# Four unnormalised feed-forward tiles and thirteen earlier modulation dots in a two-block transformer kernel

## The reference

```
h = h + merged @ w_o
hn = rmsnorm(h, ffn_norm_g)
up = causal_dwconv(hn @ w_up, ffn_conv_w, ffn_conv_b)      # 3 taps over the tokens
val, gt = split(up);  h = h + (silu(gt) * val) @ w_down
```

## Time and profile before

| | us |
|---|---|
| median of 3 runs | 2860.99 |
| lowest, highest | 2860.46, 2868.71 |
| span of the profiled execution | 2867.0 |
| PE busy in it | 2802.2 |
| DVE busy in it | 2197.3 |
| ACT busy in it | 1512.2 |

### The profile page before, as it was taken

The page is one execution under the profiler, slowest core; times in us unless marked ns, Lnnn a source line. Parts: engine busy times, 40 slices in busy tenths (PEclk is TensorE's granted clock), DMA queues, the critical chain, the costliest instruction groups (busy, mean ns, idle before and its releaser), DMA issues.

```text
span 2867.0 us, 44009 instructions
## 1 busy us (share of the span) xinstructions
PE 2802.2 (98%) x17074; PEld 2487.4 (87%) x17074; DVE 2197.3 (77%) x2750; ACT 1512.2 (53%) x1731; POOL 155.9 (5%) x226
## 2 busy tenths in 40 slices
PE   8999999999999999999999999999999999999997
PEld 8888888888888789999999989999898888788886
DVE  5645458998885899999999985655765777788887
ACT  5444564444554544544444454555544555566666
POOL 3000010000101000000000020111110000000000
PEclk9999999999999999999999999999999999999999
DMA  7444444555555788888788848444415677778885
GB/s 287 176 162 176 165 166 176 187 183 188 176 212 187 282 330 325 330 329 321 308 326 320 336 163 299 175 159 164 138 64 202 258 299 269 281 305 336 341 335 220
DMA packets 116107, 692.17 MB, mean 241 GB/s; under 512 B 14288, under 2 KB 27840, under 8 KB 35328
## 3 DMA queue, kind: packets, MB, share of 16 engines
q1 hardware_dynamic: 110384, 675.33, 62.2%
q10 hardware_dynamic: 4688, 11.01, 1.2%
q0 software_dynamic: 896, 3.93, 0.4%
HBM read 679.74 MB, written 10.49 MB: 241 GB/s over the span
## 4 chain that ended last, share of the span: by engine, by line
PE 81%; DVE 9%; ACT 4%; issue 3%; DMA 2%; SPq 0%; DVEq 0%; ACTq 0%
PE psT L1363 12%; PE psT L1350 10%; PE psT L1337 6%; PE psT L1368 6%; PE psT L1338 6%; PE psT L1339 6%; PE psT L1351 5%; DVE w_lo L2200 5%; PE psT L1480 3%; ACT w_hi L649 2%; PE psT L1977 2%; PE psT L1978 2%; PE psT L1979 2%; DMA raw<-tiles_dram 2%; PE psT L1482 1%
## 5 line engine op out<-in xcount | busy, mean ns | idle before, releaser
L2200 DVE TENSOR_TENSOR w_lo<-raw,w_hi 128x2048 fp32r<-128x2048 f32 x531 | 1216.3, 2297 | 331.8 <-ACT w_hi L649 327.2
L649 ACT ACTIVATE w_hi<-raw 128x2048 fp32r<-128x2048 f32 x531 | 1011.5, 1910 | 368.5 <-PE psT L1339 121.3
L1363 PE MATMUL psT<-a_both,w_hi 128*128 128x512 f32 x1632 | 515.9, 398 | 6.1 <-DVE a_both L2250 2.8
L1350 PE MATMUL psT<-a_both,w_hi 128*128 128x512 f32 x1440 | 511.7, 400 | 3.5 <-issue 2.6
L1351 PE MATMUL psT<-a_both,w_lo 128*128 128x256 f32 x1440 | 404.2, 281 | 0.0
L1368 PEld LDWEIGHTS psT<-a_both,w_lo 128*128 128x128 f32 x1632 | 308.1, 189 | 72.8
L1350 PEld LDWEIGHTS psT<-a_both,w_hi 128*128 128x128 f32 x1440 | 270.5, 188 | 69.1 <-issue 4.6
L1368 PE MATMUL psT<-a_both,w_lo 128*128 128x256 f32 x1632 | 321.8, 279 | 0.0
L1351 PEld LDWEIGHTS psT<-a_both,w_lo 128*128 128x128 f32 x1440 | 272.4, 189 | 0.3
L1363 PEld LDWEIGHTS psT<-a_both,w_hi 128*128 128x128 f32 x1632 | 250.2, 190 | 7.0 <-issue 4.1
L1337 PE MATMUL psT<-a_both,w_hi 128*128 128x256 f32 x784 | 228.9, 292 | 8.7 <-DVE w_lo L2373 3.1
(11 more groups left out here) (443 smaller groups left out, 4927.5 us busy)
## 6 DMA issues: line engine op xcount, KB each, us to landing
raw<-tiles_dram SPq DMA_DIRECT2D x531, 1024.0 KB, 5.3
pool<-ada_tiles_dram SPq DMA_DIRECT2D x96, 1024.0 KB, 5.1
bias_rows_dram<-pool ACTq DMA_DIRECT2D x1, 8192.0 KB, 56.8
pool<-bias_rows_dram SPq DMA_DIRECT2D x40, 128.0 KB, 4.4
raw<-tiles_dram SPq DMA_DIRECT2D x12, 256.0 KB, 7.6
pool<-bias_rows_dram SPq DMA_DIRECT2D x40, 64.0 KB, 4.6
pool<-mem_dram SPq DMA_DIRECT2D x4, 512.0 KB, 8.5
pool<-x_dram ACTq DMA_DIRECT2D x1, 2048.0 KB, 11.3
```

The costliest lines, as they stand in the source:

```text
L649: nc.scalar.activation(w_hi[:, t.k % SPL, :], raw[:, t.k % RAW, :], ACT.Copy).then_inc(hi_done, 1)
L1350: nc.tensor.matmul(dst.rearrange("p (h s) -> p h s", h=2), wh, a_both[:, :, a, :], start=first, stop=False)
L1363: nc.tensor.matmul(dst, w_hi[:, t.k % SPL, k * P:k * P + P], a_both[:, :, (k + at) % DC, :], start=k == 0, stop=False)
L2200: nc.vector.tensor_tensor(w_lo[:, t.k % SPL, :], raw[:, t.k % RAW, :], w_hi[:, t.k % SPL, :].bitcast(F32), ALU.subtract).then_inc(lo_done, 1)
```

## The change

Part one is about the modulation. Thirteen dots are made in the steps of the qm and q stages, one in each step of tiles 16 to 28, with two slots (pool chunks 24 and 64) and a silu(c) of their own (chunk 16). SP's loop over tiles 16 to 31 loads modulation tile j behind weight tile 17+j. ACT makes silu(c) behind the norm of x, and a second time in the eighth ffn tile. No dot stands in the first eight ffn tiles; nine groups have nine dots each, the last one has two.

Part two is about the start of ffn. In wo ACT rounds `h * g` into `u_hi` as well, and DVE makes its lower part (`raw_low`) once ACT has. The first four ffn tiles multiply these with `three`; DVE scales their sums by `rstd` on the way out of PSUM (`up_scaled`). The normalised pairs of `a_hi` and `a_lo` are made in four portions, in the steps of these tiles, for the tiles from the fifth on. The last squares are added up inside the first tile, and the 14 idle products are gone. In ffn SP no longer waits for the whole split ahead of the fifth tile, but ahead of the modulation loads behind the ninth.

The diff, cut to its core:

```diff
-ADA_FIRST = 6
+ADA_HEAD = 13
 ADA_EACH = 9
+ADA_LAST = 2
+ADA_LANDED = [16 * (ADA_HEAD - ADA_HEAD // 2), 16 * (ADA_HEAD // 2), 0]
...
+        u_hi = nc.alloc_sbuf_tensor_at("u_hi", [P, DC, S], F32R, offset=POOL_AT + 16 * 1024)
+        u_lo = nc.alloc_sbuf_tensor_at("u_lo", [P, DC // 2, S], F32R, offset=POOL_AT + 52 * 1024)
...
+        ADA, CROW = (0, 8, 16), 52
+        ADA_EARLY, CROW_EARLY = (24, 64), 16
...
-            load_tiles(4, BASE["glu"] + 4)
+            load_tiles(4, 16)
+            for n in range(16, 32):
+                load_tile(Tile(n))
+                j = n - 17
+                if j == 0:
+                    sp.wait_ge(W["act_lo_ready"], split_end("mem"))
+                    sp.wait_ge(W["last_squares"], 4)
+                if j == 1:
+                    sp.wait_ge(W["variance_ready"], NORM_AT["x"] + 1)
+                if 0 <= j < ADA_HEAD:
+                    wait(sp, W["ada_done"], j - 1)
+                    sp.dma_start(flat(ADA_EARLY[j % 2], 8), ada_tiles[j]).then_inc(ada_landed[j % 2], 16)
+            load_tiles(32, BASE["glu"] + 4)
...
-            sp.wait_ge(W["act_lo_ready"], split_end("ffn"))
             f0 = BASE["ffn"]
             for f in range(4, 12):
                 load_tile(Tile(f0 + f))
-                load_ada(f - 4, (f - 4) % 3)
-
-            def ffn_loads(t, i, end):
-
+                if f == 8:
+                    sp.wait_ge(W["act_lo_ready"], split_end("ffn"))
+                if f > 9:
+                    load_ada(f - 10, f - 10)
+
+            with sp.Fori(0, G1 - 2) as i:
                 for k in range(12):
-                    load_tile(t + k)
+                    load_tile(Tile(f0 + 12 + k, i, 12))
                     if ada_place(k) is not None:
-                        n = ada_place(k)
-                        if end is None or 8 + n + ADA_EACH * end < 96:
-                            j = 8 + n + (0 if end is None else ADA_EACH * end)
-                            load_ada(j, j % 3, i)
-
-            with sp.Fori(0, G1 - 2) as i:
-                ffn_loads(Tile(f0 + 12, i, 12), i, None)
-            ffn_loads(Tile(f0 + 12 * (G1 - 1)), None, G1 - 2)
+                        j = ADA_LAST + ada_place(k)
+                        load_ada(j, j % 3, i)
+            for k in range(12):
+                load_tile(Tile(f0 + 12 * (G1 - 1) + k))
...
             std("x")
+            act.wait_ge(L["crow"], 16)
+            nc.scalar.activation(flat(CROW_EARLY, 8), flat(CROW_EARLY, 8), ACT.Silu).then_inc(W["c_act"], 1)
...
                                      scale=pc("ffn_norm_g", k)).then_inc(W["pre_ready"], 1)
+                if k == 0:
+                    act.wait_ge(W["act_lo_ready"], split_end("merged"))
+                nc.scalar.activation(u_hi[:, k, :], pool[:, H + k, :], ACT.Identity, bias=zero,
+                                     scale=pc("ffn_norm_g", k)).then_inc(W["raw_hi"], 1)
             std("ffn")
-            act.wait_ge(used, BASE["ffn"])
-            hi_pairs("ffn", PRE)
...
-                    up_lower(t, k, 0, half)
+                    if n == 0:
+                        act.wait_ge(used, BASE["ffn"])
+                    if n < 4:
+                        hi_pairs("ffn", PRE, (4 * n, 4 * n + 2))
+                    else:
+                        up_lower(t, k, 0, half)
+                    if n == 7:
+                        act.wait_ge(L["crow"], 32)
+                        nc.scalar.activation(flat(CROW, 8), flat(CROW, 8), ACT.Silu).then_inc(W["c_act"], 1)
...
-            run_last("ffn", 3, SQ)
-            idle_products(14)
 
             def ffn_groups():
                 b = BASE["ffn"]
-                begin(Tile(b))
-                begin(Tile(b + 1))
-                for k in range(DC):
-                    chunk_split("ffn", k)
-                    for m in range(2):
-                        long_product(Tile(b + m), k)
-                    for m in range(2):
-                        last = short_product(Tile(b + m), k)
-                        if k == DC - 1:
-                            last.then_inc(used, 1)
-                for k in range(2, 8):
+                for m in range(4):
+                    t = Tile(b + m)
+                    begin(t)
+                    for k in range(DC):
+                        if m == 0:
+                            pe.wait_ge(W["raw_lo"], k + 1)
+                        last = three(psT[:, t.k % 2, 0:S], t, u_hi[:, k, :], raw_low(k), k, k == 0, k == DC - 1)
+                        if m == 0 and k == 6:
+                            run_last("ffn", 3, SQ)
+                    last.then_inc(used, 1)
+                wide_twos(Tile(b + 4), fresh="ffn")
+                for k in range(5, 8):
...
-            def by_pairs(name, src, rows, bias=None):
+            def by_pairs(name, src, rows, bias=None, part=range(8)):
...
-            joined("qm", 0, QM, 1.0 / 16)
+            def early_ada(j):
+
+                dve.wait_ge(ada_landed[j % 2], 16 * (j // 2 + 1))
+                buf = flat(ADA_EARLY[j % 2], 8)
+                nc.vector.tensor_tensor_reduce(out=buf, in0=buf, in1=flat(CROW_EARLY, 8), scale=1.0, scalar=0.0,
+                                               op0=ALU.mult, op1=ALU.add, accum_out=mod[:, j:j + 1])\
+                    .then_inc(W["ada_done"], 1)
+
+            dve.wait_ge(W["c_act"], 1)
+            for n in range(HC):
+                t = Tile(BASE["qm"] + n)
+                lo(t + AHEAD)
+                dve.wait_ge(W["lower_copied"], n + 1)
+                join(psT[:, t.k % 2, 0:S], pool[:, QM + n, :], 1.0 / 16)
+                early_ada(n)
             for n in range(HC):
                 t = Tile(BASE["q"] + n)
                 lo(t + AHEAD)
+                if n < ADA_HEAD - HC:
+                    early_ada(HC + n)
...
-            with dve.Fori(0, DC // 4) as i:
-                for k in range(4):
-                    t = Tile(BASE["wo"] + k, i, 4)
-                    dve.wait_ge(used, t.count())
-                    h = pool[:, bass.ds(4 * i + (H + k), 1), :]
-                    nc.vector.tensor_tensor(h, psT[:, t.k % 2, S:2 * S], h, ALU.add).then_inc(W["wo_added"], 1)
-                    dve.wait_ge(W["wo_added"], i * 4 + (k + 1))
-                    nc.vector.tensor_tensor(h, psT[:, t.k % 2, 0:S], h, ALU.add).then_inc(emptied["D"], 1)
+            for k in range(DC):
+                t = Tile(BASE["wo"] + k)
+                dve.wait_ge(used, t.count())
+                h = pool[:, H + k, :]
+                nc.vector.tensor_tensor(h, psT[:, t.k % 2, S:2 * S], h, ALU.add).then_inc(W["wo_added"], 1)
+                dve.wait_ge(W["wo_added"], k + 1)
+                nc.vector.tensor_tensor(h, psT[:, t.k % 2, 0:S], h, ALU.add).then_inc(emptied["D"], 1)
+                if k < DC - 1:
                     lo(t + AHEAD)
+                dve.wait_ge(W["raw_hi"], k + 1)
+                nc.vector.scalar_tensor_tensor(raw_low(k), h, pc("ffn_norm_g", k), u_hi[:, k, :].bitcast(F32),
+                                               ALU.mult, ALU.subtract).then_inc(W["raw_lo"], 1)
+            lo(Tile(BASE["ffn"] + 2))
             dve.wait_ge(emptied["D"], OWN[:BASE["ffn"]].count("D"))
             root("ffn", D)
             dve.wait_ge(W["pre_ready"], 16)
-            by_pairs("ffn", PRE, rstd[:, :])
-
...
+            def up_scaled(t, k):
+
+                dve.wait_ge(used, (t + k).count())
+                nc.vector.tensor_tensor(us[:, k, 2:2 + S], psT[:, (t + k).k % 2, 0:S], rstd[:, :], ALU.mult)\
+                    .then_inc(emptied["D"], 1)
...
-                    if n >= 8 - ADA_FIRST:
-                        ada_dot(n - (8 - ADA_FIRST))
+                    if n < 4:
+                        by_pairs("ffn", PRE, rstd[:, :], part=range(2 * n, 2 * n + 2))
                     if n:
                         up_taps((n - 1) % 4, 0, (n - 1) // 4)
                     if n in (3, 5, 7):
                         up_pair((n - 2) % 4, 0, (n - 2) // 4)
                     lo(Tile(b + n) + AHEAD)
-                    up_add(Tile(b + 4 * (n // 4)), n % 4, 0, n // 4)
-                ada_keep(ADA_FIRST)
+                    if n < 4:
+                        up_scaled(Tile(b), n)
+                    else:
+                        up_add(Tile(b + 4), n % 4, 0, 1)
+                dve.wait_ge(W["c_act"], 2)
...
-                            if ada_place(n) is not None:
+                            if ada_place(n) is not None and (not last or ada_place(n) < ADA_LAST):
...
+            pl.wait_ge(W["act_lo_ready"], split_end("mem"))
+            pl.wait_ge(W["last_squares"], 4)
+            pl.dma_start(flat(CROW_EARLY, 8), crow_d.partition_broadcast(P)).then_inc(L["crow"], 16)
...
-            pl.wait_ge(W["act_lo_ready"], split_end("merged"))
+            lanes("ffn", SQ, LANE)
+            pl.wait_ge(used, BASE["ffn"] + 4)
             pl.dma_start(flat(GDRAW, 2)[:, 0:384], gd_d).then_inc(L["gd"], 16)
```

(55 more changed lines are left out.)

18 lines of the change are left out of this document (5 added, 13 removed).

## The result

The change makes the kernel slower: 2947.88 us, median of four runs (2945.34 to 2951.80), against 2860.72 (2859.22 to 2868.71) for the kernel before. The ratio is 1.0299, with a 95% interval from 1.0286 to 1.0313. 2945 was predicted. In the profiled executions the span is 2950.0 us against 2867.0.

A forecast was written before the change was run, and what follows sets the result against it. TensorE (PE) was taken as the limit wherever it has no idle row. Starvation +86.5, clock +2 and feed-forward start -4.5 gave +84 us on the 2861 median: 2945 us, range 2912 to 2966.

The forecast's parts named there:

- The wait in the load queue: Query stages: SP's wait for a dot holds back weight tiles 20 to 30, lead becomes none; 86.5 us of delay.
- rival C: SP's wait doesn't hold the query stages' weights, leaving only the feed-forward start's gain: 2856.5 us; chance 0.09.
- Turn: Query stages, end of one dot to the next: load, w_hi, w_lo, join, dot in series; 13.9 us qm, 13.6 q.
- E0: End of the first early dot, where the chain of turns starts; predicted at 129.4 us.
- E7: End of the qm dots, seven turns of 13.9 us after E0; predicted at 226.8 us.
- E10: End of the dot three q turns of 13.6 us after E7; predicted at 267.6 us.
- Landing: Within a turn, the modulation and weight loads arriving: 1.8 to start, 5.0 for two MB, 0.3 to be seen; 7.1 us.
- The clock: PE restarts at half clock after idling, for 3.3 us; hidden in the turns, only the last tiles pay, 2 us.
- Rival B: PE stays at 1.2 GHz through the query stages, a tile lasting 10.6 us: 2960 us; chance 0.12.
- Part 2: Feed-forward start: unnormalised first tiles gain 3.2 us and lag behind dots at 1010.92 and 1018.04 goes, 1.5: 4.7 us.
- The dots at nothing beside PE: Query stages: thirteen dots of about 2.3 us each on DVE fit beside PE's tiles and cost nothing.

The follow-up runs named there:

- e1_lead4: Changed kernel with SP issuing modulation tile j behind weight tile 21+j, not 17+j, so four tiles of lead; 2858.44 us, ratio 0.9977.
- the second execution: The changed kernel run again unchanged, in the second study; 2944.39 us, ratio 1.0295.
- e3_small: Changed kernel with each of the 13 early modulation loads cut from 1 MB to 128 KB, all waits kept; 2933.25 us, ratio 1.0245.
- e2_lead1: Changed kernel with SP issuing modulation tile j behind weight tile 18+j, not 17+j, so one tile of lead; 2875.94 us, ratio 1.0050.
- e5_scaled_first: e1_lead4 with `up_scaled` moved to the start of each of DVE's first four feed-forward steps, from behind w_lo; 2848.19 us, ratio 0.9954.
- e4_part1: Kernel before plus only part one, with e1_lead4's load order and the old feed-forward start; 2857.58 us, ratio 0.9982.

## Why the prediction was right

**The wait in the load queue** was the cause. e1_lead4 shows it by moving that wait alone, and rival C falls with it. The delay was predicted as 86.5 + 2 and is 91 at tile 31.
- Turn: 13.9 us in qm and 13.6 in q predicted, 14.18 on average measured (14.07 in the second execution). E0 is 128.1, not 129.4; E7 227.0 against 226.8; E10 269.9 against 267.6. The turn into the memory attention, 226.97 to 242.31, is 15.3 us, the next two 13.8. In it w_hi starts 8.9 us after the issue (226.97 to 235.84) and not 7.5; why is open.
- Landing: 7.5 against 7.1. I had 1.8 us to start, 5.0 for two MB and 0.3 to be seen; the windows beside e3_small have the first data at 129.00, 0.9 us after the issue, a slow first 1.75 us, then 424 GB/s, which is 2.5 us for each MB, until 134.75, and w_hi starts 0.8 later. So the price of a MB was right, and what was short by 0.4 is the fixed part: 2.5 us and not 2.1.
- Behind E10 the attention products ahead of tile 30 take 3.0 us (293.43 to 296.45), where I had counted 1.0. With the 2.3 at E10 this is why tile 31 is 4.4 behind the predicted 300. The two us that I had added for the clock are in here: the eight attention products take 3.58 us at 293.43, after 3.06 idle, and 1.89 at 280.39.

**The clock.** The first product of a starved tile is 0.77 us long in place of 0.47. The first such tile lasts 7.3 us (140.27 to the beginning of the idle time before 154.42), as predicted, but the next two 8.6 and 8.5. Windows in the kernel after:

```profile
172.00:174.00 2.00, 2.00 (x7) 1.71 (x7) 0.00 (x0) 0.00 (x0) 0.00 (x0) 0.50 0.77 328
...
174.50:176.50 2.00, 2.00 (x13) 1.77 (x12) 0.00 (x0) 0.00 (x0) 0.00 (x0) 1.00 1.02 430
```

PE waited 5.44 us before 168.43 and works at 0.50, the 1.2 GHz level, until 174, and then at full clock; over 150 to 200 the mean is 0.71. The clock comes back within each tile, but later than the 3.3 us that I had read from the earlier trace rows in most of them. So the idle time before a tile is not some 8 us but 8.5 once and then 4.5 to 6.8. The Trainium skill ("TensorE: Matmul & The Clock Gate", section "HAM oscillation — how this bites in real kernels") says that tiles which each wait for a DMA start cold every time. It agrees for the ten tiles or attention ticks from 140.27 to 270.38, which PE reached after 4.5 to 8.5 us idle and began with a product of 0.76 or 0.77 us; the tile at 284.05, after 1.76 us, began at full clock. Rival B, a whole tile at half rate, does not hold: a tile is 7.3 to 8.6 and not 10.6 us, and is hidden in the turn.

**Part 2.** The starts of tiles 2 to 5 came within 0.2 us. The gain of 4.7 was measured as 5.1, but that is in part luck. I gave 3.2 to the unnormalised products and 1.5 to the dots that left; up to the thirteenth up tile the products give 2.7 and the dots 3.7, and the rest of the stage loses 1.3, which I had not foreseen. The step that failed is the sizing of DVE's lag by the idle rows at 1010.92 and 1018.04. Those say 1.52 us, but while DVE is late PE's neighbouring products seem to be spread as well: 55 of them start from 1005 to 1015, and 59 in the ten us before. Where exactly the rest lies was not measured.

**The dots at nothing beside PE.** True in qm, not in q: there the step on DVE is 8.7 us with a dot in it, over PE's 7.3. In the kernel after this is hidden below the turn. It was a step I missed, though it hardly moved this forecast, and it shows where the lead is one tile (e2_lead1).

## What to carry to other kernels

Before a wait is put into an in-order load queue, write down for each load behind it which instruction it now waits for and how many tiles ahead of use that is: a lead of zero turned load, w_hi, w_lo, join and dot into one serial chain, at 14 us a tile where PE needs 5.5, though from 150 to 200 no engine was busy for more than about 57% of the time. One tile of lead brought back 68.5 of 83 us, four tiles brought all, at no cost in memory. When products are started ahead of their scale factor, free PSUM first in every step, since the engines that make the next operands wait behind that emptying: this order was worth 7.5 us in its stage (e5_scaled_first), the early products without it about 1.

## What the runs showed that was not expected

PE's pace in the same code at full granted clock is one of two. Windows from 600 to 700 in the kernel before, then in e1_lead4; the code of this stage is the same in both:

```profile
600.00:700.00 100.00, 100.00 (x568) 86.81 (x567) 90.27 (x126) 44.80 (x54) 8.06 (x3) 1.00 0.51 186
```

```profile
600.00:700.00 100.00, 100.00 (x579) 87.44 (x578) 92.02 (x131) 47.73 (x57) 8.08 (x3) 1.00 0.53 189
```

568 products in one and 579 in the other, 2%. The pace doesn't hold everywhere: from 413 to 775 it is 2042 in the kernel before, 2055 in e1_lead4 and 2066 in e4_part1, which is worth 2 to 4 us. The kernel after has the first pace in both of its profiles, the five kernels of the experiments the second. What sets it is open. It makes a single execution a poor judge of 5 us, which is why the parts of the feed-forward stage were compared from marker to marker.

A strip of a tile is not cheap in proportion to its bytes. The difference of 1.7 us for 7/8 MB (e3_small) seems to say that a second MB in the queue costs 2.0 us, but the strip that is left costs more than its share. By the rate of 424 GB/s in the kernel after a whole second MB costs 2.5 us, the same as in the earlier trace rows.
